# The head of the expert stage: two query pieces multiplied beside the shifts, modulation rows after them, and the first head's top-k one token tile at a time

## The reference

```
def peer_ffn(u, w_q, sub_keys, expert_u, expert_v):        # u: 256 tokens x 1024
    q = (xc @ w_q).reshape(tc, PEER_HEADS, 2, PEER_DQ // 2)        # 8 heads x 2 x 128
    s = jnp.einsum('thpd,hpkd->thpk', q, sub_keys)                 # 128 scores per half
    s_top, i_top = lax.top_k(s, PEER_TOPK)                         # 16 of 128
    cand = s_top[:, :, 0, :, None] + s_top[:, :, 1, None, :]       # 16 x 16 sums
    cand_idx = i_top[:, :, 0, :, None] * PEER_NKEYS + i_top[:, :, 1, None, :]
    best, pos = lax.top_k(cand.reshape(...), PEER_TOPK)            # 16 of 256
    expert = take_along_axis(cand_idx, pos)                        # a row number
    gate = softmax(best)
    ue, ve = expert_u[expert], expert_v[expert]                    # 2 x 1024 floats a row
    h = gelu(einsum('thkd,td->thk', ue, xc))
    return einsum('thk,thkd->td', gate * h, ve)
```

## Time and profile before

| what | value |
|---|---|
| median of 3 runs | 1447.61 us |
| profiled execution | 1454.04 us |
| its span | 1452.2 us |
| PE busy | 1239.3 us (85%) |
| DVE busy | 911.7 us (63%) |
| ACT busy | 408.1 us (28%) |
| POOL busy | 274.1 us (19%) |
| bytes moved by DMA | 428.30 MB |

### The profile page before, as it was taken

One profiled execution on the slowest core, in us unless ns is written; L12 is line 12 of the kernel. 1 busy time (PEld: TensorE's weight loads), 2 busy tenths in 40 slices (PEclk: granted clock), 3 DMA queues, 4 the chain that ended last, 5 costly groups with the idle time before them and its releaser, 6 DMA issues. The chain is left out here.

```text
span 1452.2 us, 20054 instructions
## 1 busy us (share of the span) xinstructions
PE 1239.3 (85%) x7874; PEld 844.9 (58%) x7874; DVE 911.7 (63%) x2012; ACT 408.1 (28%) x866; POOL 274.1 (19%) x264
## 2 busy tenths in 40 slices
PE   4898998768888878888887777879998988899898
PEld 1888858533333324333332222369995678899898
DVE  0694245777887868787877865673337665555452
ACT  2551224411110201111010100163453353544431
POOL 0000000054443444444443343200000000000000
PEclk8899999989999999999999999999999979999999
DMA  9366089399999999999999999765444733355543
GB/s 395 130 232 181 4 329 428 147 412 421 421 421 421 421 422 421 421 415 419 418 404 421 422 408 421 322 252 200 179 174 184 286 147 138 116 183 192 195 151 121
DMA packets 50764, 428.30 MB, mean 295 GB/s; under 512 B 5744, under 2 KB 7920, under 8 KB 8304
## 3 DMA queue, kind: packets, MB, share of 16 engines
q0 software_dynamic: 36864, 268.45, 44.7%
q1 hardware_dynamic: 13808, 158.59, 28.3%
HBM read 423.64 MB, written 1.05 MB: 292 GB/s over the span
## 5 line engine op out<-in xcount | busy, mean ns | idle before, releaser
L1325 PE MATMUL bank<-arena 128*128 128x512 f32 x1024 | 499.0, 615 | 119.0 <-DVE arena L1469 118.9
L1325 PEld LDWEIGHTS bank<-arena 128*128 128x128 f32 x1024 | 176.5, 190 | 426.6 <-DVE arena L1469 285.2
L480 PE MATMUL bank<-rounded,rounded 128*128 128x256 f32 x1256 | 370.5, 295 | 46.1 <-DVE rounded L443 32.6
L1511 DVE CUSTOM_DVE_ANT_0 arena<-arena 128x1024 f32<-128x1024 f32 x256 | 313.6, 1225 | 148.3 <-DMA arena<-experts_in,arena 145.2
L1248 POOL DMA_INDIRECT arena<-experts_in,arena x256 | 273.6, 1069 | 618.9 <-PE bank L1325 353.2
L481 PE MATMUL bank<-rounded,rounded 128*128 128x256 f32 x1256 | 362.8, 289 | 0.0
L482 PE MATMUL bank<-rounded,ring_r 128*128 128x256 f32 x1256 | 362.1, 288 | 0.0
L457 DVE TENSOR_TENSOR ring_r<-ring,rounded 128x1024 fp32r<-128x1024 f32 (+2 forms) x151 | 189.1, 1264 | 144.3 <-ACT rounded L452 144.0
L480 PEld LDWEIGHTS bank<-rounded,rounded 128*128 128x128 f32 x1256 | 248.4, 198 | 52.2 <-issue 29.3
L481 PEld LDWEIGHTS bank<-rounded,rounded 128*128 128x128 f32 x1256 | 248.4, 198 | 3.0 <-issue 2.9
L482 PEld LDWEIGHTS bank<-rounded,ring_r 128*128 128x128 f32 x1256 | 248.2, 198 | 0.0
(11 more groups left out here) (246 smaller groups left out, 933.2 us busy)
## 6 DMA issues: line engine op xcount, KB each, us to landing
ring<-slots_in SPq DMA_DIRECT2D x68, 2048.0 KB, 8.4
arena<-slots_in SPq DMA_DIRECT2D x4, 2048.0 KB, 23.8
arena<-experts_in,arena POOLq DMA_INDIRECT x256, 13.6
xT<-xT_in SPq DMA_DIRECT2D x1, 1024.0 KB, 11.0
mixT<-slots_in SPq DMA_DIRECT2D x1, 1024.0 KB, 11.9
out_dram<-xT SPq DMA_DIRECT2D x1, 1024.0 KB, 3.9
arena<-slots_in SPq DMA_DIRECT2D x1, 896.0 KB, 7.0
uT<-arena SPq DMA_DIRECT2D x4, 142.0 KB, 9.4
```

What stands on the lines that cost most here:

```text
L480: pe.matmul(dst, hi[:, k, :], xh, start=(k == 0), stop=False)
L1325: ins = pe.matmul(psum[2 * tt + half][:, :], diag[:, r % DIAGS, :], rows[:, r % GRING, D + 512 * half:D + 512 * half + 512], start=(h == 0 ...
L1511: dve.tensor_tensor_reduce(rows[:, r % GRING, 0:D], rows[:, r % GRING, 0:D], utok[:, tt, :], 1.0, 0.0, ALU.mult, ALU.add, hdot[:, r:r + 1] ...
```

## The change

Four things are changed at the head of the expert stage. Query pieces 0 and 1 are no longer split: PE multiplies the plain float32 weight by the plain float32 input, one feature tile at a time, directly behind that tile's shift and ahead of its transposes (`PLAIN = 2`; the Split now has 14 pieces, so its indices are lower by two). Both halves of `pe_mod(pe, 3, ...)` now stand behind `piece(3)`. ACT makes all eight shifts first, then the rounded copies. And head 0's top-k is done for token tile 0 first, with its own `tk_expert`, then `dve_lo` of the piece that `piece(3)` multiplies, then token tile 1; POOL waits for the tile's own mark.

```
         PLAIN = 2
         wq = Split([... for i in range(PLAIN, NHP)], KT, uT, 2048, wq_mm, buffers=4)
 POOL
                 pool.wait_ge(early_used, 4)
                 for h in range(HEADS):
-                    pool.wait_ge(tk_expert, h + 1)
                     for tt in range(TT):
+                        pool.wait_ge(tk_expert, h + 2 if h else tt + 1)
 PE
-                pe_mod(pe, 3, 0, 4)
+                wait_slot(pe, SLOTS["w_q"][0])
                 for k in range(KT):
                     pe.wait_ge(nm_shift, shifted[0] + k + 1)
+                    for i in range(PLAIN):
+                        ins = pe.matmul(psum[4 + i][:, 0:T], slot(SLOTS["w_q"][0])[:, k, i * P:(i + 1) * P], uT[:, k, :],
+                                        start=(k == 0), stop=(k == KT - 1))
+                        if k == KT - 1:
+                            ins.then_inc(wq_mm, 1)
                     for tt in range(TT):
                         ins = pe.transpose(...)
-                piece(0)
-                piece(1)
                 scores(0)
                 piece(2)
                 piece(3)
-                pe_mod(pe, 3, 4, KT)
+                pe_mod(pe, 3, 0, KT)
                 pe_mod_cols(pe, 3)
 ACT
-                ffn_norm.act(act, wq)
-                wq.act_hi(act, 3)
+                ffn_norm.act_rstd(act)
+                for k in range(KT):
+                    act.wait_ge(nm_n, KT * NORMED + k + 1)
+                    act.activation(uT[:, k, :], uT[:, k, :], ACT.Identity, bias=...).then_inc(nm_shift, 1)
+                for k in range(0, KT, 2):
+                    wq.act_x_pair(act, k)
+                wq.act_hi(act, 0)
                 q_out(0)
                 q_out(1)
                 ... (four copies of the transposed input)
-                wq.act_hi(act, 4)
-                wq.act_hi(act, 5)
+                for i in range(1, 4):
+                    wq.act_hi(act, i)
 DVE
-                ffn_norm.dve(dve, wq)
-                wq.dve_lo(dve, 3)
-                for s in range(5):
-                    key_step(0, s)
-                candidates()
-                ...
-                experts(0)
-                dve_mod(dve, 3).then_inc(mod2_read, 1)
-                wq.dve_lo(dve, 4)
-                wq.dve_lo(dve, 5)
+                ... (the eight scalings)
+                wq.dve_x(dve)
+                wq.dve_lo(dve, 0)
+                dve.wait_ge(ut_mm, TT)
+                dve.wait_ge(split_xlo, wq.xbase + KT // 2)
+                for tt in range(TT):
+                    ts = slice(tt, tt + 1)
+                    for s in range(5):
+                        key_step(0, s, ts)
+                    candidates(ts)
+                    for s in range(5):
+                        cand_step(s, ts)
+                    if tt:
+                        shares(0)
+                    dve.wait_ge(tk_ready, count[0])
+                    for half in range(2):
+                        decode(half, 0, ts)
+                        decode(half, 1, ts)
+                    experts(0, ts)
+                    if tt == 0:
+                        wq.dve_lo(dve, 1)
+                dve_mod(dve, 3).then_inc(mod2_read, 1)
+                wq.dve_lo(dve, 2)
+                wq.dve_lo(dve, 3)
```

More of the change, by code:

```diff
@@ L1207, in build @@
                                                                                        "ms", "var"))
-        wq = Split([(SLOTS["w_q"][0] + i // 4, 512, (i % 4) * P, i) for i in range(NHP)], KT, uT, 2048, wq_mm,
+        PLAIN = 2
+        wq = Split([(SLOTS["w_q"][0] + i // 4, 512, (i % 4) * P, i) for i in range(PLAIN, NHP)], KT, uT, 2048, wq_mm,
                    buffers=4)
+        NORMED = norms[0] - 1
         def q_tile(i):
@@ L1254, in piece @@
                 def piece(i):
[L1255 to L1257 removed]
+                    pe.wait_ge(wq_ev, i - 1)
+                    wq.pe_products(pe, i - PLAIN, psum[4 + i % 2][:, 0:T]).then_inc(wq_mm, 1)
                 def scores(h):
@@ L1347, in squares @@
                                        scale=D ** -0.5).then_inc(px_sq, 1)
-                ffn_norm.act(act, wq)
-                wq.act_hi(act, 3)
+                ffn_norm.act_rstd(act)
+                for k in range(KT):
+                    act.wait_ge(nm_n, KT * NORMED + k + 1)
+                    act.activation(uT[:, k, :], uT[:, k, :], ACT.Identity, bias=mod1[:, 24 + k:25 + k]).then_inc(nm_shift, 1)
+                for k in range(0, KT, 2):
+                    act.wait_ge(nm_shift, shifted[0] + k + 2)
+                    wq.act_x_pair(act, k)
+                shifted[0] += KT
+                wq.act_hi(act, 0)
                 q_out(0)
@@ L1416, in top_step, with shape, key_step @@
                         count[0] += 1
-                def key_step(h, s):
-                    if s == 0:
+                both = slice(0, TT)
+                def shape(ts):
+                    return [P, ts.stop - ts.start, TOPK, TOPK]
+                def key_step(h, s, ts=both):
+                    if s == 0 and ts.start == 0:
                         dve.wait_ge(sc_mm, h + 1)
@@ L1422, in key_step, with candidates, cand_step @@
                             dve.sem_inc(slot_used[(SLOTS["w_q"][0] + h // 2) % RING], 1)
-                    top_step(s, lambda j: psum[6 + h % 2][:, j * NKEYS:(j + 1) * NKEYS], lambda j: work[:, j, :],
-                             lambda j: top[:, j // 2, j % 2, :], lambda j: topu[:, j // 2, j % 2, :], 2 * TT)
-                def candidates():
-                    dve.wait_ge(tk_ready, count[0])
[L1428 to L1436, removed]
+                    first = 2 * ts.start
+                    top_step(s, lambda j: psum[6 + h % 2][:, (first + j) * NKEYS:(first + j + 1) * NKEYS],
+                             lambda j: work[:, first + j, :],
+                             lambda j: top[:, ts.start + j // 2, j % 2, :], lambda j: topu[:, ts.start + j // 2, j % 2, :],
+                             2 * (ts.stop - ts.start))
+                def candidates(ts=both):
+                    dve.wait_ge(tk_ready, count[0])
+                    if ts.stop == TT:
+                        dve.sem_inc(sc_used, 1)
+                    v(dve.tensor_copy(topi[:, ts], topu[:, ts]))
+                    v(dve.tensor_tensor(cand[:, ts].rearrange("p t (a b) -> p t a b", a=TOPK),
+                                        top[:, ts, 0, :].unsqueeze(3).to_broadcast(shape(ts)),
+                                        top[:, ts, 1, :].unsqueeze(2).to_broadcast(shape(ts)), ALU.add))
+                def cand_step(s, ts=both):
+                    t0 = ts.start
+                    top_step(s, lambda j: cand[:, t0 + j, :], lambda j: cwork[:, t0 + j, :], lambda j: best[:, t0 + j, :],
+                             lambda j: posu[:, t0 + j, :], ts.stop - t0)
                 def shares(h):
@@ L1441, in shares, with decode, experts @@
                                       ALU.subtract).then_inc(tk_best, 1)
-                def decode(half, part):
+                def decode(half, part, ts=both):
                     op, by = ((ALU.logical_shift_right, 4), (ALU.bitwise_and, 15))[half]
                     if part == 0:
[L1446 to L1449, removed]
-                    else:
[L1451 to L1456, removed]
+                        v(dve.tensor_scalar(half_u[:, ts], posu[:, ts], by, None, op))
+                        v(dve.tensor_copy(half_f[:, ts], half_u[:, ts]))
+                        v(dve.tensor_tensor(hot[:, ts], half_f[:, ts].unsqueeze(3).to_broadcast(shape(ts)),
+                                            cst("iota").unsqueeze(1).unsqueeze(1).to_broadcast(shape(ts)), ALU.is_equal))
+                    else:
+                        v(dve.tensor_tensor(hot[:, ts], hot[:, ts], topi[:, ts, half, :].unsqueeze(2).to_broadcast(shape(ts)),
+                                            ALU.mult))
+                        v(dve.tensor_reduce(pick[:, half, ts], hot[:, ts], AX_X, ALU.add))
+                def experts(h, ts=both):
+                    v(dve.scalar_tensor_tensor(pick[:, 0, ts], pick[:, 0, ts], float(NKEYS), pick[:, 1, ts], ALU.mult, ALU.add))
+                    dve.tensor_copy(picked(expert, h)[:, ts], pick[:, 0, ts]).then_inc(tk_expert, 1)
                 def gates(h):
@@ L1484, in gain_squares @@
                                                  xT[:, k, half_tile(tt)], ALU.mult, ALU.mult).then_inc(px_gsq, 1)
-                ffn_norm.dve(dve, wq)
-                wq.dve_lo(dve, 3)
-                for s in range(5):
-                    key_step(0, s)
-                candidates()
[L1491 to L1496, removed]
-                experts(0)
-                dve_mod(dve, 3).then_inc(mod2_read, 1)
-                wq.dve_lo(dve, 4)
-                wq.dve_lo(dve, 5)
+                dve.wait_ge(nm_rstd, 2 * NORMED + 2)
+                for k in range(KT):
+                    dve.scalar_tensor_tensor(uT[:, k, :], xT[:, k, :], gain[:, 1, k:k + 1], rstd[:],
```

(4 more changed lines are left out.)

8 lines of the change are left out of this document (4 added, 4 removed).

## The result

The changed kernel takes 1454.26 us (median of 7 runs, 1450.35 to 1459.36), the kernel before 1447.67 us (7 runs, 1445.52 to 1450.32). The ratio is 1.0044, with a 95% interval of 1.0029 to 1.0060: 6.6 us slower. The forecast was 1453.9, within 1449 to 1458.5.

A forecast was written before the change was run, and what follows sets the result against it. The prediction took gather DMA to bound the expert loop; top-k, remainder, piece 3, modulation rows and reaction put the first gather 6.3 us later, so 1447.6 + 6.3 = 1453.9 us, range 1449 to 1458.5.

The forecast's parts named there:

- The bound: Expert loop: gathers moving 268.45 MB at 420 GB/s take 639 us, so a later first gather delays the end equally.
- Which mark decides: First gather: GpSimd waits for `tk_expert` and `early_used`; the later decides, now `early_used` from TensorE's modulation rows, at 293.8.
- top-k starts earlier by: Head 0's top-k on VectorE: start between 269.7 and 271.4, taken as 270.5, against 271.57 before.
- clock behind the first rest: TensorE's dense products after 2.4 us of rest: loss from half clock taken as 0.85 us, bounds 0 and 3.4.
- first tile, top-k to row numbers: VectorE's top-k for token tile 0: 9.6 us, or 7.7 if all halves, 11.2 if decoding gains nothing.
- remainder, to piece 3's start: VectorE's remainder behind tile 0's row numbers: 1.2 us, so TensorE's piece 3 can start at 281.4.
- piece 3 and rows, at the clock as it was: TensorE's piece 3 and eight modulation steps: 10.1 us at full clock plus 2.35 for half clock, 12.4.
- GpSimd's reaction: From the deciding mark to the first gather: 0.5 us, between 0.28 after TensorE and 0.9 after VectorE.
- first gather later by: Start of GpSimd's first gather: 294.3 against 287.96, 6.3 us later.
- The faster one: Rival, 10%: piece 3 doesn't wait for its remainder, gather 3.7 to 5.4 us earlier, about 5 us faster (1443).
- The larger loss: Rival, 20%: both TensorE clock costs at upper bound and half the tile's bound, about 9.5 us slower (1457).
- Made up in the loop: No-change rival, 10%: slack at the loop's beginning absorbs the late first gather, leaving 1447.6 us.

The follow-up runs named there:

- rest filled: Changed kernel plus four extra plain products, results unused, in TensorE's rest ahead of the first shift; 1452.67 us, ratio 1.0032.
- the repeated kernel: Changed kernel with the eight modulation steps between pieces 2 and 3, timed a second time without any edit; 1441.53 us, ratio 0.9954.
- rows before piece 3: Changed kernel with the eight modulation steps moved from behind piece 3 to between pieces 2 and 3 on TensorE; 1439.30 us, ratio 0.9942.
- remainder early: Changed kernel with the rounded copy and remainder for piece 3 made ahead of head 0's top-k; 1443.17 us, ratio 0.9967.
- token tiles only: Kernel before with only the token-tile order of head 0's top-k and GpSimd's finer marks; 1443.05 us, ratio 0.9965.
- whole top-k: Changed kernel with head 0's top-k done for both tiles at once and piece 3's remainder behind it; 1458.96 us, ratio 1.0075.
- two steps in the rest: Changed kernel with two modulation steps ahead of the shifts and the other six between pieces 2 and 3; 1440.14 us, ratio 0.9951.
- remainders later: Kernel of two steps in the rest, with remainders for pieces 4 and 5 behind head 0's first and ninth dot products; 1442.46 us, ratio 0.9966.

## Why the prediction was right

*The bound.* The step "each microsecond at the first gather is one at the end" is the one on which all else rests. Over the kernels up to the rest filled, the first gather moved by 19 us, from 24.35 to 43.32, and the distance stayed within 650.8 and 651.5, the repeated kernel apart. The medians, against the kernel before beside them, follow the gather: -8.7 (rows before piece 3), -4.8 (remainder early), -4.9 (token tiles only), +6.6 (changed) and +11.0 us (whole top-k) for -6.6, -4.2, -5.8, +5.9 and +12.4 at the gather (the repeated kernel: -6.6 for -6.7). Each of these shifts lies inside the 95% interval of its ratio. What held is that the distance stays, not its size: the prediction's 639 us, bytes by rate, left out that the first row takes 5.8 us to arrive and that the DMA engines are used at 0.82 in the first ten microseconds; measured it is 651.

*Which mark decides.* Right, and shown from both sides: the first gather is released by the modulation rows, and taking away either the late remainder or the position of the rows behind piece 3 removes the whole loss.

*The terms.* From L293, forecast against measured:

| term | forecast | measured |
|---|---|---|
| top-k starts earlier by | 1.05 (1.9 to 0.2) | 0.88 |
| clock behind the first rest | 0.85 (0 to 3.4) | 3.4 us at 0.50, so 1.7 |
| first tile, top-k to row numbers | 9.6 | 9.66 |
| remainder, to piece 3's start | 1.2 | 1.23 |
| piece 3 and rows, at the clock as it was | 12.4 | 11.94 |
| GpSimd's reaction | 0.5 | 0.32 |
| first gather later by | 6.3 | 5.88 |

The start of the top-k came out right partly by luck, as two errors nearly cancel. The clock did fall behind the 2.4 us of rest, in the changed kernel and in all four other runs with the same order there, for 3.4 us each; I had taken half of that. But the plain products were cheaper: the pace in the trace is 1.08 us per feature tile (258.86, 259.94, 261.02, ...), where 2 x 0.45 + 2 x 0.15 = 1.20 had been taken from whole groups, whose last record runs on after the next instruction could start (four plain records last 1.03 us, and the transposes start 0.86 behind their start). Eight times 0.12 is 1.0, which pays for most of the clock. And the keys landed at 12.1 and not at the 11.4 of the prediction, so without the loss of clock the scores could have started only some 0.2 us earlier. Piece 3 and the rows came in 0.5 below the forecast, as piece 3 lost 1.9 us at 0.50 and not 2.35. The candidate steps went as the rows had suggested: they start 0.54 apart (270.25 to 270.79) where a match load stands between and 0.44 where none does (271.32 to 271.76), and last 0.41 to 0.43 each, so they do wait for one another. Of a pair in the kernel before, which don't need each other's result, the second starts 0.39 behind the first with a match load between them, while the first still runs:

```profile
278.25 0.42 DVE L1408 FIND_INDEX8 uT<-uT 128x8 uint32<-128x256 f32 x1
278.58 0.07 DVE L1408 MATCH_VALUE_LOAD uT<-uT 128x8 f32 x1
278.64 0.42 DVE L1408 FIND_INDEX8 uT<-uT 128x8 uint32<-128x256 f32 x1
```

By the Trainium skill ("VectorE: DVE Perf Modes", the DRAIN you can't avoid), which measured plain copies, the semaphore would have cost nothing; the five steps took 2.5 us where half of the pairs' time is 1.9. Here the measurement decides, against the rule as it was applied.

*The other rule.* The Trainium skill's port pair ("SBUF — State Buffer", the "DVE blocks DMA" trap) made the reaction nearer to 0.3 when VectorE rests. It was 0.32. The trace agrees with the number, but two runs speak against the reason. In the kernel with token tiles only, VectorE went from the row numbers straight to selections that read the scores' bank, one input and not two from SBUF, and GpSimd still took 0.93. With the remainder early, VectorE was in tile 1's selections when the gather started (a MAX8 runs from 279.27 to 279.70, the gather starts at 279.34), and GpSimd took 0.32 all the same. So VectorE need not rest for the 0.3. No run here sets an operation with two inputs from SBUF against a wait that TensorE ends, so what the port itself costs stays open.

*The rivals.* The faster one was priced at 3.7 to 5.4 us earlier at the gather, if piece 3 did not wait for its remainder. That is the kernel with the remainder early: 4.2, released by the modulation rows as the rival said. The mechanism and price were right, its condition was not met by the change. The larger loss (both clock costs at their bound) did not come: 5.9 at the gather. Its terms, 6.3, 2.55, 1.05 and 0.8, make 10.7 and not 10. "Made up in the loop" was false: in the changed kernel too the share of DMA is 1.01 from ten microseconds after the gather's start.

## What to carry to other kernels

An event with two waits has a second-latest one that no profile row names; before moving work away from the visible one, find when the silent one comes and what the edit does to it. Here, moving 3.6 us of filler work past a piece, and that piece's operand past a selection, made an area's release come 12.7 us later (36.5 in place of 23.8), and nobody had been waiting for it before. Put what frees a buffer ahead of what merely needs an operand. And when the loop behind is bound by bytes, compare offsets from the last unchanged point, not spans: the spans here differed by 0.3 us while the loop started 5.9 later.

## What the runs showed that had not been expected

GpSimd's first gather starts 0.92 to 0.93 us after VectorE's row numbers when these come last (before, token tiles only, two steps in the rest, remainders later), and 0.31 to 0.33 after TensorE's last modulation matmul when that comes last (changed, remainder early, rest filled, whole top-k). In the kernel with the rows before piece 3 the profile names TensorE, whose rows ended 0.07 us behind the row numbers (23.49 and 23.42), but the gather came 0.93 after the row numbers: it was most likely VectorE's mark that released it. The cause of the difference of 0.6 us stays open.

The keys let the scores start only 11.8 to 12.1 us behind L293 in the three kernels with a filled rest, where 256.5 + 11.9 in the kernel before had given 11.4. Beyond that point an earlier start of the scores needs the keys earlier.

Whether a rest makes the clock fall can't be told from its length alone. In the kernel with two steps in the rest piece 3 follows a rest of 2.88 us and 3.4 us at 0.50 begin 1.3 us into it; with the remainders later the rest is 2.87 us and the clock stays at 1.00. The same stretch in the two, 1.3 and 0.8 us behind piece 3's start:

```profile
278.80:282.20 3.40, 3.14 (x16) 2.85 (x14) 3.08 (x15) 0.22 (x1) 2.67 (x3) 0.50 0.90 304
278.80:282.20 3.40, 2.45 (x22) 2.25 (x20) 3.12 (x18) 0.86 (x2) 2.49 (x4) 1.00 0.77 246
```
